# Gated recurrence: the diagonal and the two smallest levels of the pairwise decay become one step over blocks of four tokens

## The reference

```python
bcum = jnp.cumsum(gc, axis=2)
diff = bcum[:, :, :, None, :] - bcum[:, :, None, :, :]
decay = jnp.where(causal, jnp.exp(jnp.where(causal, diff, 0.0)), 0.0)
attn = jnp.sum(qc[:, :, :, None, :] * kc[:, :, None, :, :] * decay, axis=-1)
o = einsum(attn, vc) + einsum(qc * jnp.exp(bcum), state)
```

## Time and profile before

| what | value |
| --- | --- |
| time, median of 3 runs | 1040.75 us (1040.24 to 1041.43) |
| profiled execution | 1040.38 us |
| its span, first to last instruction | 1038.5 us |
| mean granted TensorE clock | 0.992 |
| busy: PE, weight loads, DVE, ACT, POOL | 98%, 82%, 62%, 50%, 28% |

### The profile page before, as it was taken

One profiled execution on the slowest core, in us unless ns is written; L12 is line 12 of the kernel. 1 busy time (PEld: TensorE's weight loads), 2 busy tenths in 40 slices (PEclk: granted clock), 3 DMA queues, 4 the chain that ended last, 5 costly groups with the idle time before them and its releaser, 6 DMA issues.

```text
span 1038.5 us, 15307 instructions
## 1 busy us (share of the span) xinstructions
PE 1015.2 (98%) x6388; PEld 856.0 (82%) x6388; DVE 641.0 (62%) x838; ACT 517.5 (50%) x804; POOL 287.1 (28%) x144
## 2 busy tenths in 40 slices
PE   7789999999999999999999999999999999999997
PEld 6669899888888888888888889988888888888876
DVE  5786884899645445355547779479983353444552
ACT  5846665675462323232447667477656333332333
POOL 1111111542422314143212111163243232323420
PEclk9889999999999999999999999999999999999999
DMA  6422222212223232333243222122231232323602
GB/s 217 133 81 66 74 67 82 81 45 79 82 65 118 81 102 87 96 102 122 88 136 112 82 82 82 42 82 82 81 102 62 81 102 81 102 81 102 198 5 81
DMA packets 93412, 94.71 MB, mean 91 GB/s; under 512 B 2256, under 2 KB 91552, under 8 KB 93344
## 3 DMA queue, kind: packets, MB, share of 16 engines
q1 hardware_dynamic: 93216, 93.70, 29.0%
q10 hardware_dynamic: 128, 0.04, 0.0%
HBM read 91.64 MB, written 2.10 MB: 90 GB/s over the span
## 4 chain that ended last, share of the span: by engine, by line
PE 93%; DVE 3%; ACT 2%; issue 1%; DMA 1%; SPq 0%; DVEq 0%; ACTq 0%
PE pj L500 27%; PE pj L502 26%; PE pj L501 26%; PE mx L635 2%; PE mx L500 1%; PE mx L501 1%; PE mx L502 1%; PE mx L575 1%; PE mx L598 1%; PE mx L695 1%; ACT w_hi L810 1%; PE mx L663 1%; PE mx L583 1%; PE mx L673 1%; DVE w_lo L1256 1%
## 5 line engine op out<-in xcount | busy, mean ns | idle before, releaser
L1146 POOL TENSOR_TENSOR w_lo<-w_raw,w_hi 128x1024 fp32r<-128x1024 f32 (+1 forms) x89 | 195.5, 2197 | 579.8 <-ACT w_hi L810 579.5
L500 PE MATMUL pj<-h_hi,w_hi 128*128 128x512 f32 x832 | 330.3, 397 | 0.0
L502 PE MATMUL pj<-h_hi,w_lo 128*128 128x512 f32 x832 | 324.6, 390 | 0.0
L501 PE MATMUL pj<-h_lo,w_hi 128*128 128x512 f32 x832 | 324.5, 390 | 0.0
L810 ACT ACTIVATE w_hi<-w_raw 128x1024 fp32r<-128x1024 f32 (+1 forms) x180 | 160.1, 939 | 162.6 <-PE pj L502 162.5
L1256 DVE TENSOR_TENSOR w_lo<-w_raw,w_hi 128x1024 fp32r<-128x1024 f32 (+1 forms) x91 | 165.2, 1815 | 74.1 <-ACT w_hi L810 73.8
L500 PEld LDWEIGHTS pj<-h_hi,w_hi 128*128 128x128 f32 x832 | 156.8, 188 | 34.4 <-issue 2.6
L502 PEld LDWEIGHTS pj<-h_hi,w_lo 128*128 128x128 f32 x832 | 156.5, 188 | 33.1
L501 PEld LDWEIGHTS pj<-h_lo,w_hi 128*128 128x128 f32 x832 | 156.7, 188 | 32.2 <-issue 1.0
L1353 DVE TENSOR_TENSOR merge_gate<-pj,rstd 128x512 f32<-128x512 f32 x48 | 33.2, 692 | 162.9 <-PE pj L502 162.9
L920 ACT ACTIVATE merge_gate<-merge_gate,small 128x512 f32<-128x512 f32 x48 | 34.3, 715 | 89.3 <-DVE merge_gate L1353 89.3
(11 more groups left out here) (255 smaller groups left out, 1494.7 us busy)
## 6 DMA issues: line engine op xcount, KB each, us to landing
w_raw<-in_w_in SPq DMA_DIRECT2D x61, 1024.0 KB, 5.5
w_raw<-in_w_branch SPq DMA_DIRECT2D x24, 512.0 KB, 3.4
w_raw<-in_w_out SPq DMA_DIRECT2D x6, 1024.0 KB, 5.1
x_tokens<-in_x SPq DMA_DIRECT2D x4, 512.0 KB, 7.2
w_raw_last<-in_w_out SPq DMA_DIRECT2D x2, 1024.0 KB, 7.3
w_raw<-in_w_in SPq DMA_DIRECT2D x2, 512.0 KB, 6.2
sp_w_rows<-in_sp_w SPq DMA_DIRECT2D x2, 512.0 KB, 5.5
out<-out_low SPq DMA_DIRECT2D x4, 256.0 KB, 2.0
```

Of the source, the lines that this page charges most:

```text
L500: pe.matmul(bank, wh, ah, start=first, stop=False)
L501: pe.matmul(bank, wh, al, start=False, stop=False)
L502: return pe.matmul(bank, wl, ah, start=False, stop=final)
L1146: return pool.tensor_tensor(out=dst, in0=full, in1=hi.bitcast(f32), op=ALU.subtract)
```

## The change

The levels go from seven to five. The diagonal, level 5 and level 6 become one step over blocks of four tokens: `block4_diffs` (DVE) forms the doubled difference from the block's middle, `block4_exp` (ACT) takes two exponentials of it, `block4_operands` (DVE) scales all keys and all queries (the latter into a new buffer `HQ`), `diagonal` (PE) multiplies them with as many matmuls as before, and `take_block4` (DVE) clears all of `AT` and copies by a mask. The visits at d+7 are gone. Everything that is placed by d + LEVELS comes two steps earlier relative to d: for p = 0 `states` goes from phase 23 to 21, `recurrent_out` from hook 23 to 21, `recurrent_evac` from phase 24 to 22, `head_norm` from hook 24 to 22, `head_rstd` and `head_scaled` from phase 25 to 23. For p = 1 `block4_diffs` and `block4_exp` stand in phase 23 too, behind these, and `block4_operands` in phase 24, ahead of the diffs of levels 0 and 1, which now both stand there. DIAG and the places of B's work are as before. The core of the diff (left out: the masks in the constants, the counts of the semaphores and the changed index of a mask):

```diff
@@ -61,9 +61,10 @@
 SG_JOBS = [n for n in range(NJ) if KIND[n] in ("ag", "bu", "bg", "cg")]
 GATE_JOBS = [n for n in SG_JOBS if KIND[n] != "bu"]
 BRANCH = {"ag": 0, "bg": 1, "cg": 2}
-LEVELS = 7
+LEVELS = 5
 DIAG = (12, 25)
-PAIRS = ((0,), (1, 2), (3, 4), (5, 6))
+MASKS = 16 + 8 * (LEVELS - 1)
+PAIRS = ((0,), (1, 2), (3, 4))
 
 ATTN = 7
 ROPE_AT = (2, 3, 4, 5, 6)
...
@@ -168,6 +172,7 @@
         r_sg = region(4)
         SG = at("gate", [P, 2, T], r_sg)
         QR = at("q_raw", [P, 3, T], r_sg)
+        HQ = [at(f"query_blocks{p}", [P, 2 * T], r) for p, r in enumerate((r_sg, r_scr + 12 * KB))]
         TT = at("full", [P, 2, T], r_tt := region(4))
         KS = at("k_groups_swapped", [P, T], r_tt + 2 * KB)
         CST = at("consts", [P, NC_], region(NC_ * 4 / KB))
...
@@ -601,22 +608,20 @@
 
 
                 def diagonal(p):
-                    evacuated(pe, FIRST[("cq", p)] + 1, layer)
-                    pe.wait_ge(c_keys, upto(c_keys, p + 1))
+                    pe.wait_ge(ops_ready, upto(ops_ready, (LEVELS + 1) * p + 1))
                     if p == 1:
                         pe.wait_ge(oc_rstd, upto(oc_rstd, 1))
                     for hb in range(2 * TB):
-                        hh, tb = divmod(hb, TB)
                         for half in range(2):
                             rows = slice(half * 64, half * 64 + 64)
-                            b = slice(tb * P + half * 64, tb * P + half * 64 + 64)
-                            last = pe.matmul(M[4][rows, hb * 64:(hb + 1) * 64], KK[p][:, hh, b], QC[p][:, hh, b],
+                            b = slice(hb * P + half * 64, hb * P + half * 64 + 64)
+                            last = pe.matmul(M[4][rows, hb * 64:(hb + 1) * 64], XL[1][:, b], HQ[p][:, b],
                                              start=True, stop=True)
                     last.then_inc(lev_done, 1)
 
                 def level(p, lev):
                     s = 64 >> lev
-                    pe.wait_ge(ops_ready, upto(ops_ready, LEVELS * p + lev + 1))
+                    pe.wait_ge(ops_ready, upto(ops_ready, (LEVELS + 1) * p + lev + 2))
                     ops = XL[lev % 2]
                     bank = M[3 + lev % 2]
                     if lev == 0:
...
@@ -954,13 +959,18 @@
                                               bias=lb[:, h:h + 1], scale=oml[:, h:h + 1])
                     last.then_inc(logf_ready, 1)
 
+                def block4_exp(p):
+                    act.wait_ge(diff_done, upto(diff_done, (LEVELS + 2) * p + 1))
+                    act.activation(E[1][:, :], E[0][:, :], ACT.Exp, scale=0.5)
+                    act.activation(E[0][:, :], E[0][:, :], ACT.Exp, scale=-0.5).then_inc(decay_ready, 1)
+
                 def decay_exp(p, lev):
-                    act.wait_ge(diff_done, upto(diff_done, (LEVELS + 1) * p + lev + 1))
+                    act.wait_ge(diff_done, upto(diff_done, (LEVELS + 2) * p + lev + 2))
                     act.activation(E[lev % 2][:, :], E[lev % 2][:, :], ACT.Exp).then_inc(decay_ready, 1)
 
                 def block_exp(p):
-                    act.wait_ge(diff_done, upto(diff_done, (LEVELS + 1) * (p + 1)))
-                    act.wait_ge(ops_ready, upto(ops_ready, LEVELS * (p + 1)))
+                    act.wait_ge(diff_done, upto(diff_done, (LEVELS + 2) * (p + 1)))
+                    act.wait_ge(ops_ready, upto(ops_ready, (LEVELS + 1) * (p + 1)))
                     act.activation(E[1][:, 0:6 * P], E[1][:, 0:6 * P], ACT.Exp)
                     act.activation(E[0][:, :], BC[p][:, :, :].rearrange("p h t -> p (h t)"), ACT.Exp)\
                        .then_inc(decay_ready, 1)
...
@@ -1089,9 +1099,9 @@
                     phase[ATTN + 1 + 3 * j].append((softmax_exp, j))
                 for p, d in enumerate(DIAG):
                     phase[FIRST[("cf", p)] + 2].append((forget, p))
-                    for i, levels in enumerate(PAIRS):
-                        for lev in levels:
-                            phase[d - 1 + max(lev if i < 2 else 2 * i, 0)].append((decay_exp, p, lev))
+                    phase[d - 2].append((block4_exp, p))
+                    for lev in range(LEVELS):
+                        phase[d + (-1, -1, 1, 3, 3)[lev]].append((decay_exp, p, lev))
                     phase[d + LEVELS].append((block_exp, p))
                     phase[d + LEVELS + 3].append((khatT_out, p))
                     phase[d + LEVELS + 5].append((recurrent_evac, p))
...
@@ -1450,51 +1460,64 @@
                 def halves(a, s):
                     return a.rearrange("p (b u s) -> p b u s", u=2, s=s)
 
+                def block4_diffs(p):
+
+                    if p == 0:
+                        dve.wait_ge(rope_done, upto(rope_done, 5))
+                    else:
+                        dve.wait_ge(state_ready, upto(state_ready, 1))
+                    b = BC[p][:, :, :].rearrange("p h t -> p (h t)").rearrange("p (b u) -> p b u", u=4)
+                    mid2 = E[1][:, 0:2 * T // 4]
+                    chained(dve.tensor_tensor(out=mid2, in0=b[:, :, 1], in1=b[:, :, 2], op=ALU.add))
+                    dve.scalar_tensor_tensor(out=E[0][:, :].rearrange("p (b u) -> p b u", u=4), in0=b, scalar=2.0,
+                                             in1=mid2.unsqueeze(2).to_broadcast([P, 2 * T // 4, 4]),
+                                             op0=ALU.mult, op1=ALU.subtract).then_inc(diff_done, 1)
+
+                def block4_operands(p):
+                    dve.wait_ge(decay_ready, upto(decay_ready, (LEVELS + 2) * p + 1))
+                    if p == 1:
+                        dve.wait_ge(lev_done, upto(lev_done, LEVELS + 1))
+                        dve.wait_ge(oc_done, upto(oc_done, 1))
+                    dve.tensor_tensor(out=XL[1][:, :], in0=KK[p][:, :, :].rearrange("p h t -> p (h t)"),
+                                      in1=E[0][:, :], op=ALU.mult)
+                    evacuated(dve, FIRST[("cq", p)] + 1, layer)
+                    dve.tensor_tensor(out=HQ[p][:, :], in0=QC[p][:, :, :].rearrange("p h t -> p (h t)"),
+                                      in1=E[1][:, :], op=ALU.mult).then_inc(ops_ready, 1)
+
                 def diffs(p, lev):
                     s = 64 >> lev
                     b = halves(BC[p][:, :, :].rearrange("p h t -> p (h t)"), s)
                     e = halves(E[lev % 2][:, :], s)
 
-                    if (p, lev) == (0, 0):
-                        dve.wait_ge(rope_done, upto(rope_done, 5))
-                    elif lev >= 2:
-                        dve.wait_ge(ops_ready, upto(ops_ready, LEVELS * p + lev - 1))
-                    elif p == 1:
-                        dve.wait_ge(state_ready, upto(state_ready, 1))
+                    dve.wait_ge(ops_ready, upto(ops_ready, (LEVELS + 1) * p + max(lev, 1)))
                     mid = b[:, :, 0, s - 1:s].to_broadcast([P, 1024 // (2 * s), s])
                     dve.tensor_tensor(out=e[:, :, 0, :], in0=mid, in1=b[:, :, 0, :], op=ALU.subtract)
                     dve.tensor_tensor(out=e[:, :, 1, :], in0=b[:, :, 1, :], in1=mid, op=ALU.subtract).then_inc(diff_done, 1)
 
                 def operands(p, lev):
                     s = 64 >> lev
-                    n = LEVELS * p + lev
-                    dve.wait_ge(decay_ready, upto(decay_ready, (LEVELS + 1) * p + lev + 1))
-                    if n >= 2:
-
-                        q, back = divmod(n - 2, LEVELS)
-                        dve.wait_ge(lev_done, upto(lev_done, (LEVELS + 1) * q + back + 2))
+                    dve.wait_ge(decay_ready, upto(decay_ready, (LEVELS + 2) * p + lev + 2))
+                    if p + lev > 0:
+                        dve.wait_ge(lev_done, upto(lev_done, (LEVELS + 1) * p + lev))
                     e, o = halves(E[lev % 2][:, :], s), halves(XL[lev % 2][:, :], s)
                     k, q = (halves(a[p][:, :, :].rearrange("p h t -> p (h t)"), s) for a in (KK, QC))
                     dve.tensor_tensor(out=o[:, :, 0, :], in0=k[:, :, 0, :], in1=e[:, :, 0, :], op=ALU.mult)
-                    if lev == 0:
-                        evacuated(dve, FIRST[("cq", p)] + 1, layer)
                     dve.tensor_tensor(out=o[:, :, 1, :], in0=q[:, :, 1, :], in1=e[:, :, 1, :], op=ALU.mult)\
                        .then_inc(ops_ready, 1)
 
-                def take_diagonal(p):
+                def take_block4(p):
                     dve.wait_ge(lev_done, upto(lev_done, (LEVELS + 1) * p + 1))
                     if p == 0:
                         dve.wait_ge(rope_done, upto(rope_done, 5))
                     else:
                         dve.wait_ge(oc_ready, upto(oc_ready, 1))
                     at4 = AT[:, :, :].rearrange("p h (b t) -> p (h b) t", t=P)
-                    dve.memset(at4[64:128, :, 0:64], 0.0)
+                    chained(dve.memset(AT[:, :, :], 0.0))
                     for half in range(2):
                         rows = slice(half * 64, half * 64 + 64)
```

(57 more changed lines are left out.)

## The result

The changed kernel takes 1045.38 us (median of 12 runs) against 1035.9 us for the kernel before on the same chips (12 runs): ratio 1.0087, 95% interval 1.0067 to 1.0107. It is slower.

What follows compares the result with a forecast made beforehand. PE, busy 98% of the span, was taken as the bound: 1040.4 - 7.9 (matmuls) + 2 x 6.3 (waits) + 2 x 1.9 (clock) = 1048.9, forecast 1049 us. Own range 1046.5 to 1051.5, wide range 1041 to 1052.

Steps and rivals of the forecast that it cites:

- The matmuls: On PE, the visits with levels 5 and 6 go and the new diagonal adds 0: -7.9 us in two layers.
- The early part: p = 0, phases 10 to 18: nothing late for PE, taken at 0, up to 1 us a layer.
- The collision: Phases 22 to 24: the low part of unit 13 comes late for job 26; PE waits 6.3 us a layer.
- The open point: In phase 23, whether POOL holds `head_scaled` with both inputs in SBUF; taken as blocked, otherwise 1.42 us for both.
- The first rival: In phase 23, POOL doesn't hold `head_scaled`; low part 1.7 us late, 1035.9 us; chance 0.10.
- The clock: On PE behind the new wait, the lower clock of 0.50 costs 1.9 us a layer, bounds 0 and 2.3.
- Sum: Whole kernel: 1040.4 - 7.9 + 2 x 6.3 + 2 x 1.9 = 1048.9 us, 1049 for the median.
- the base of 1040.4 us: Whole kernel before: time of the profiled execution the terms were added to, 0.4 us under the median of runs shown.
- Nothing late: At the collision, DVE, ACT and POOL all arrive in time for PE: 1032.5 us; chance 0.06.
- a smaller lateness: At job 26, POOL's part isn't in DVE's way: 3.9 us late a layer, 1043.3 us; chance 0.06.
- the clock stays: At job 26, PE's wait comes but its clock isn't lowered: 1045.1 us; chance 0.12.
- The further wait: Another PE wait, at the early transposes or p = 1's levels behind the collision: 1050 to 1053 us; chance 0.08.

Runs made afterwards that it cites:

- DIAG (12, 27): The changed kernel with the recurrence of p = 1 two steps later; 1028.86 us, ratio to the kernel before 0.9927.
- the guarded kernel before: The kernel before, with POOL's low part of the unit split at job 6 waiting for the last rope product; 1035.59 us.
- the short `ln_affine`: The changed kernel with POOL's `ln_affine` on only the first 128 of 512 tokens; lower group 1028.3 to 1028.9 us, ratio 0.9939.

## Why the prediction was right, and where its level was off

*The matmuls.* Forecast -7.9 us. The changed kernel has 512 records of the levels instead of 768, and where nothing is late afterwards the gain is 6.5 to 6.8 us. PE's busy time is 7.6 us shorter (1006.5 with DIAG (12, 27) against 1014.1 in the guarded kernel before, both with the long spell at the lower clock near the start). PE waits 0.9 us for the last rope product in the one and 0.3 for POOL in the other; about 0.5 us stays unplaced. Right.

*The early part.* Taken at 0; PE has no wait there in any profile.

*The collision.* Right link by link: `layer_norm_scale` late by the operations put ahead of `ln_rsqrt`, `head_scaled` held until the second affine ended, `block4_diffs(1)`, the exponentials, the gate, `split_hi(13)`, POOL's turn within DVE's diffs, the low part. In the upper group's time PE was to ask at 201.5 us and get the low part at 207.8; in this execution of the lower group it asked at 196.4 and got it at 202.9. Forecast 6.3 us a layer, measured 6.5. The open point was the form: `SCALAR_TENSOR_TENSOR` with both inputs in SBUF is held like the differences of rows 5 (7.42 us for two). The first rival falls with it. The rule of the Trainium skill ("SBUF — State Buffer", "Who interferes with whom") for two SBUF inputs agrees with this row too.

*The clock.* Forecast 1.9 us a layer. It was at 0.50 for 4.2 us after the wait in layer 0 and for 5.0 in layer 1, which makes 2.1 and 2.5; keeping PE busy gave back 2.4 a layer. So 0.8 us of the difference lie here. The price taken from rows 9 isn't a fixed one: behind the wait of 5.6 us near the start, PE ran at 0.50 for 2.94 us in the execution shown and for 5.56 (41.02 to 46.58) in the changed kernel's.

*Sum.* The terms as measured, 13.0 of waits and 4.6 of clock less 7.9 of matmuls, make +9.7 us. Forecast +8.5 on the execution shown, measured +9.4 group against group.

*The level.* 1049 us against 1045.38, off by 3.6: the step that failed is the base of 1040.4 us. I took PE's 4.4 us wait for the last rope product, and the lower clock behind it, as a fixed part of the kernel; the runs show it in some executions only (four of the twelve of the kernel before), and the lower group of that kernel has its median at 1035.6. The base was 4.8 us too high and the change 0.9 too small, and the rest is that the median of all twelve runs lies 0.4 above that of their lower group. The forecast's own range of 1046.5 to 1051.5 missed the median by this, the wide one held it. Where the median falls is partly luck: the first three runs were all of the upper group, and had most of the later runs been of it (the changed kernel's median there is 1050.2), the level would have been 1.2 us too low instead.

*The rivals.* Nothing late, a smaller lateness: both fall by the wait of 6.5 us; the clock stays: by the stretch at 0.50. The further wait didn't come.

## What to carry to other kernels

Where one engine is the bound and the others run by a handwritten order, removing its work is the easy half; the placed steps that come forward with it land in other company. Look at what POOL runs in that stretch: here a POOL instruction of some 5 us held the next DVE instruction with two SBUF inputs until it ended (7.42 us for two instead of 1.42) and, through it, every engine that waited for DVE. Put first what the bounding engine asks for next (here the low part of the weights), and try the moved group one and two places later before giving it up: two steps made +9.4 us into -6.5 to -6.8. And when the times of a kernel form two groups, look for such a meeting before you take one execution's wait as a fixed cost.

## What the runs showed of the hardware

A meeting of one DVE instruction with one POOL instruction, won or lost by less than 0.6 us, made two groups of times 5 us apart: in the upper group DVE's last rope product starts 0.3 to 0.5 us behind POOL's split, in the lower it ends 0.1 to 0.4 us ahead of it. A fixed order took the upper group away. Of the two groups' distance the wait makes 3.3 us (4.4 less 1.1). The lower clock behind the longer wait adds 2.3, and the shorter spell of it near the start takes 1.3 back; some 0.8 us stay unplaced. A wait of 1.1 us left PE's clock at 1.00, waits of 4.4 to 6.6 us didn't; the spell at 0.50 behind them was 2.9 to 6.1 us long (6.1 with the short `ln_affine`, near the start), and waits of the same length had spells of different length.
